# A two-layer decoder trunk on one Trainium2 core: the first two gate and up tile pairs by direct block products

## What is computed

```python
def rmsnorm(x, g):
    y = xf * lax.rsqrt(jnp.mean(xf * xf, axis=-1, keepdims=True) + EPS)
    return (y * g).astype(x.dtype)

def swiglu(x, wg, wu, wd):
    return (jax.nn.silu(x @ wg) * (x @ wu)) @ wd

h = h + 0.5 * swiglu(rmsnorm(h, norm_ffn1), ffn1_gate, ffn1_up, ffn1_down)   # 1024 -> 2816 -> 1024
```

## Time and profile before

| | |
|---|---|
| times of three runs | 2783.46, 2786.13, 2786.66 us |
| span of the profiled execution | 2784.5 us |
| TensorE busy | 2759.6 us, 99% of the span |
| VectorE busy | 1983.0 us, 71% |
| ScalarE busy | 1193.2 us, 43% |
| granted TensorE clock, mean | 0.999 |
| HBM read and written | 291.51 MB and 30.94 MB |

### The profile page before, as it was taken

One profiled execution on the slowest core, in us unless ns is written; L12 is line 12 of the kernel. 1 busy time (PEld: TensorE's weight loads), 2 busy tenths in 40 slices (PEclk: granted clock), 3 DMA queues, 4 the chain that ended last, 5 costly groups with the idle time before them and its releaser, 6 DMA issues.

```text
span 2784.5 us, 58089 instructions
## 1 busy us (share of the span) xinstructions
PE 2759.6 (99%) x22004; PEld 2677.3 (96%) x22004; DVE 1983.0 (71%) x3581; ACT 1193.2 (43%) x2139; POOL 128.3 (5%) x233
## 2 busy tenths in 40 slices
PE   8999999999999999999999999999999999999999
PEld 7999999998899999999999999999888999999999
DVE  8889534478767688887488895344787576899952
ACT  6445323435424254444254453234354333544521
POOL 0000001230000000000000000012300000000000
PEclk9999999999999999999999999999999999999999
DMA  4222325463335312223212222165723343122233
GB/s 140 92 96 96 108 75 198 158 203 127 108 109 191 122 61 91 90 91 121 84 69 90 90 105 100 68 206 159 226 107 119 106 179 130 62 96 100 99 106 104
DMA packets 104929, 326.02 MB, mean 117 GB/s; under 512 B 15055, under 2 KB 31967, under 8 KB 103216
## 3 DMA queue, kind: packets, MB, share of 16 engines
q1 hardware_dynamic: 91872, 280.75, 28.9%
q0 software_dynamic: 12880, 42.84, 4.7%
HBM read 291.51 MB, written 30.94 MB: 116 GB/s over the span
## 4 chain that ended last, share of the span: by engine, by line
PE 96%; DVE 2%; ACT 1%; issue 0%; DMA 0%; SPq 0%; DVEq 0%; ACTq 0%
PE ps L1442 51%; PE ps L1493 35%; PE ps L1679 3%; PE ps L1748 1%; PE ps L1961 1%; PE ps L1798 1%; PE ps L1779 1%; PE ps L1454 0%; PE ps L1826 0%; PE ps L1846 0%; PE ps L1730 0%; PE ps L1467 0%; DMA hT<-h_in 0%; PE ps L1788 0%; PE ps L1461 0%
## 5 line engine op out<-in xcount | busy, mean ns | idle before, releaser
L2121 DVE TENSOR_TENSOR w_lo<-w_raw,w_hi 128x1024 fp32r<-128x1024 f32 x240 | 292.7, 1223 | 345.2 <-ACT w_hi L829 341.6
L1493 PE MATMUL ps<-x_more,w_hi 128*128 128x296 f32 (+1 forms) x2112 | 456.8, 298 | 2.2 <-DVE x_more L2993 1.4
L1493 PE MATMUL ps<-x_hi,w_hi 128*128 128x296 f32 (+1 forms) x1408 | 420.5, 299 | 2.4 <-DVE w_lo L2159 2.4
L1493 PE MATMUL ps<-x_hi,w_lo 128*128 128x296 f32 (+1 forms) x1408 | 421.0, 299 | 0.0
L1493 PE MATMUL ps<-x_lo,w_hi 128*128 128x296 f32 (+1 forms) x1408 | 420.9, 299 | 0.0
L829 ACT ACTIVATE w_hi<-w_raw 128x1024 fp32r<-128x1024 f32 x224 | 235.0, 1053 | 407.2 <-PE ps L1442 240.1
L1442 PE MATMUL ps<-x_hi,w_hi 128*128 128x296 f32 (+1 forms) x1600 | 362.8, 308 | 3.8 <-ACT hT L1175 3.8
L2159 DVE TENSOR_TENSOR w_lo<-w_raw,w_hi 128x512 fp32r<-128x512 f32 x440 | 296.4, 689 | 88.9 <-ACT w_hi L877 86.5
L1493 PEld LDWEIGHTS ps<-x_more,w_hi 128*128 128x128 f32 x2112 | 350.7, 188 | 3.6 <-issue 2.1
L1442 PE MATMUL ps<-x_hi,w_lo 128*128 128x296 f32 (+1 forms) x1600 | 346.6, 298 | 0.0
L1442 PE MATMUL ps<-x_lo,w_hi 128*128 128x296 f32 (+1 forms) x1600 | 346.5, 298 | 0.0
(11 more groups left out here) (381 smaller groups left out, 4882.2 us busy)
## 6 DMA issues: line engine op xcount, KB each, us to landing
w_raw<-wstream SPq DMA_DIRECT2D x420, 512.0 KB, 3.8
kpage<-cache_k SPq DMA_DIRECT2D x128, 128.0 KB, 3.0
vpage<-cache_v POOLq DMA_DIRECT2D x128, 128.0 KB, 3.8
gate_rows<-hT SPq DMA_DIRECT2D x48, 296.0 KB, 3.0
d_sg<-gate_rows SPq DMA_DIRECT2D x16, 888.0 KB, 4.8
h_rows<-hT SPq DMA_DIRECT2D x2, 2368.0 KB, 9.6
hT<-h_rows SPq DMA_DIRECT2D x2, 2368.0 KB, 10.2
hT<-h_in SPq DMA_DIRECT2D x4, 592.0 KB, 8.4
```

Of the source, the lines that this page charges most:

```text
L1493: mm = pe.matmul(ps[:, bank, 0:span()], wp[:, k, :], xp, start=new and k == 0 and n == 0, stop=k == KH - 1 and n == 2, skip_group_check=True)
L2121: v.tensor_tensor(w_lo[:, slot, :, :], w_raw[:, slot, :, :], w_hi[:, slot, :, :].bitcast(F32), ALU.subtract).then_inc(weights_low, 1)
```

## The change

It touches layer 0's first SwiGLU alone.

- Pairs 0 and 1 are each made by direct block products: gate tile and up tile, 8 channel tiles, 3 passes, 2 token halves, 96 matmuls a pair in place of 84. For pair 0 this goes tile by tile (k = 0 to 7) as input tiles and weight pieces arrive. A new operand B12 is kept for it.
- The input is loaded tile by tile (8 loads in place of 4), and the first two weight units in four pieces that each hold two channel tiles of both (1024 contiguous bytes in place of 4096).
- The input array holds a second copy of h with tokens on partitions (five windows of 80 or 128 tokens by 1024). SP loads it behind the rest. ScalarE squares and sums its rows (an accumulator), takes Ln and Exp of the sums; VectorE multiplies an identity by them (diagonals), TensorE multiplies by ones to spread them over partitions, ScalarE copies the result out. The 14 matmuls on square_rooms and the 2 on ssum go.
- TensorE waits, ahead of pair 2's first product, for `pair_steps`, which VectorE's direct_rate(1) raises. Pair 2 then takes the seven-product scheme; pairs 2 and 3 stand written out, the loop starts at pair 4.
- POOL issues the constants after the input has arrived; the bias rows are made behind pair 2.

```diff
+DIRECT = 2
+            def load_chunk(c):
+                sp.dma_start(chunk(w_raw, c), wstream[0:2].rearrange("a p (k m) -> p a k m", k=8)[:, :, 2 * c:2 * c + 2, :]
+                             ).then_inc(chunk_load(c)[0], 16)
+            load_tile(0)
             sp.dma_start(prm[:, :], params[0][:, 0:NP_ - P]).then_inc(h_loaded[0], 16)
+            for c in range(4):
+                load_chunk(c)
+                load_tile(2 * c + 1)
+                if c < 3:
+                    load_tile(2 * c + 2)
+            load_first(2)
+            load_tokens(0)
+            load_first(3)
+            for w in range(1, WINDOWS):
+                load_tokens(w)
             sp.wait_ge(consts_loaded, 16 * CONSTS)
...
+            pl.wait_ge(h_loaded[3], TILE_COUNT[3])
+            pl.dma_start(ident[:, :], c_ident).then_inc(consts_loaded, 16)
...
+            def opening_inverse():
+                act.wait_ge(tokens_loaded, 16 * WINDOWS)
+                for w in range(WINDOWS):
+                    n = window(w)[1]
+                    act.activation(tokens[0:n, w, :], tokens[0:n, w, :], ACT.Square, accum_out=token_squares[0:n, w:w + 1]
+                                   ).then_inc(squared, 4 if w == WINDOWS - 1 else 1)
...
+            def opening_pairs():
+                for k in range(KD):
+                    for u in range(2):
+                        mm = direct_block(0, u, k)
+                        if k == KD - 1:
+                            mm.then_inc(products_done, 3 + u)
+                for p in range(1, DIRECT):
+                    for u in range(2):
+                        pe.wait_ge(weight_steps, W_STEPS * p + (W_STEPS if u else 5))
+                        if p == 1 and u:
+                            pe.wait_ge(norm_steps, 2)
+                        elif p > 1:
+                            pe.wait_ge(pair_steps, PAIR_STEPS * p + (6 if u else 4))
+                        for k in range(KD):
+                            if p == 1 and u == 0 and k == KD - 2:
+                                opening_inverse()
+                            mm = direct_block(p, u, k)
+                        mm.then_inc(products_done, 3 + u)
...
+                if opening:
+                    opening_pairs()
+                    pe.wait_ge(pair_steps, PAIR_STEPS * (DIRECT + 1) + 4)
+                    begin(DIRECT, DIRECT % 2)
+                    for n in range(DIRECT, 4):
+                        pair_(n, n % 2, "opening" if n == DIRECT else "steady")
+                        if n == DIRECT:
+                            bias_rows()
...
+            def opening_ffn():
...
+                diagonal_roots()
+                for k in range(KH):
+                    opening_low("T1", k, kept_rooms[:, k, 0, :], gain_of(P_GAIN, k))
+                v.wait_ge(norm_steps, 2)
+                direct_rate(0)
...
+                direct_gate(0)
+                direct_hidden(0)
...
+                for k in range(KH):
+                    opening_low("T2", k, difference_rooms(0, k)[0], None)
...
+                for k in range(KH):
+                    opening_low("T3", k, difference_rooms(0, k)[1], None)
...
+                sum_one(g, w_sum)
+                low(N, W_A11, g, w_sum)
...
+                sum_three(N, g)
+                low(N, W_S1, g, w_sum)
+                sum_two(N, g, w_sum)
+                sum_four(N, g, w_sum)
+                low(N, W_S2, g, w_sum)
+                for k in range(KH):
+                    fourth(0, k, P_GAIN, opened("T2", k))
+                low(N, W_S4, g, w_sum)
+                direct_rate(last)
+                for k in range(KH):
+                    opening_low("T4", k, difference_rooms(0, k)[0], None)
```

More of the change, by code:

```diff
@@ L993, in ffn @@
                 quad0 = l * QUADS + first // RING
-                pair_(N0, quad0, 0, "first", 0)
-                pair_(N0 + 1, quad0, 1, "steady", 1)
-                with act.Fori(1, KF // 2 - 1) as i:
+                opening = l == 0 and f == 0
+                if opening:
+                    opening_ffn()
+                    for n in range(DIRECT, 4):
+                        pair_(N0 + n, quad0 + n // 2, n % 2, "steady", n)
+                        if n == DIRECT:
+                            bias_rows()
+                else:
+                    pair_(N0, quad0, 0, "first", 0)
+                    pair_(N0 + 1, quad0, 1, "steady", 1)
+                with act.Fori(2 if opening else 1, KF // 2 - 1) as i:
                     for j in range(2):
@@ new lines, in opening_inverse @@
+            def opening_inverse():
+                pe.wait_ge(consts_loaded, 16 * CONSTS)
+                pe.wait_ge(squares_summed, 8)
+                for w in range(WINDOWS):
+                    c0, n = window(w)
+                    bank, c = (6, c0) if w < WINDOWS - 1 else (7, 0)
+                    mm = pe.matmul(ps[:, bank, c:c + n], ones[0:n, 0, :], diagonals[0:n, w, 0:n], start=True, stop=True)
+                mm.then_inc(square_total, 1)
+            def opening_pairs():
[11 more added lines that the diff above has]
+                            pe.wait_ge(pair_steps, PAIR_STEPS * p + (6 if u else 4))
+                        for k in range(KD):
+                            if p == 1 and u == 0 and k == KD - 2:
+                                opening_inverse()
+                            mm = direct_block(p, u, k)
+                        mm.then_inc(products_done, 3 + u)
@@ L1484, in ffn, with bias_rows @@
+            def bias_rows():
+                pe.wait_ge(bias_row_moved, 32)
+                for bank, c in ((2, 0), (3, 512), (6, 1024)):
+                    mm = pe.matmul(ps[0:16, bank, 0:min(512, RL - c)], rb[0:33, :], bucket[0:33, c:min(c + 512, RL)], start=True, stop=True)
+                mm.then_inc(bias_row_made, 1)
             def ffn(l, f, first):
@@ L1498, in operand @@
                     pe.wait_ge(weight_steps, W_STEPS * N + W_LOW[t])
+                opening = l == 0 and f == 0
                 def x_operand(t):
-                    pe.wait_ge(x_parts, parts(l, f, t, KH - 1))
+                    pe.wait_ge(x_parts, OPENING_PARTS.index((t, KH - 1)) + 1 if opening else parts(l, f, t, KH - 1))
                 def begin(N, j):
@@ L1509, in pair_ @@
                 def pair_(N, j, kind):
-                    first_ = kind == "first"
+                    first_ = kind in ("first", "opening")
                     operand(N, W_S1)
@@ L1545, in fifth @@
                         product(W_A12, BANK_B, True)
-                    if first_ and l == 0 and f == 0:
-                        opening_squares()
-                    if first_:
+                    if kind == "first":
                         fifth()
@@ L2092, in _ @@
             pe.sem_inc(units_multiplied, RING)
-            pe.wait_ge(bias_row_moved, 32)
-            for n, c in enumerate(range(0, RL, 512)):
-                mm = pe.matmul(ps[0:16, 5 + n, 0:min(512, RL - c)], rb[0:33, :], bucket[0:33, c:min(c + 512, RL)], start=True, stop=True)
-            mm.then_inc(bias_row_made, 1)
             for l in range(DEPTH):
@@ L3140, in layouts @@
     h = np.concatenate([a["x_sample"].reshape(TS, D), a["meta_tokens"], a["x_prompt"].reshape(SEQ, D)], axis=0)
-    out["h_in"] = h.T.reshape(KD, P, T).transpose(1, 0, 2)
+    rows = np.zeros((P, WINDOWS, D), f)
+    for w in range(WINDOWS):
+        c0, n = window(w)
+        rows[0:n, w] = h[c0:c0 + n]
+    out["h_in"] = np.concatenate([h.T.reshape(KD, P, T).transpose(1, 0, 2).reshape(P, KD * T), rows.reshape(P, WINDOWS * D)], axis=1)
     units = []
```

345 lines of the change are left out of this document (209 added, 136 removed).

## The result

| | before | changed |
|---|---|---|
| median of runs side by side | 2785.93 us (14 runs, 2782.93 to 2788.70) | 2792.45 us (14 runs, 2789.43 to 2794.73) |
| profiled execution: span | 2784.5 us | 2789.1 us |
| granted clock, mean of the span | 0.999 | 0.996 |

The ratio is 1.0026 with a 95% interval of 1.0019 to 1.0033: slower by 6.5 us in the median. That is more than the 5.6 us (0.2%) under which the prediction took a change for none, though the lower end of the interval, 0.19%, lies just under that mark. The prediction expected 2787.7 us, in a range of 2781.5 to 2792: 1.6 us slower than before. It was wrong: the median lies 0.45 us above its range, and the loss is four times the one that it forecast.

A forecast was written before the change was run, and what follows sets the result against it. TensorE, busy 99% of the span, was taken as the bound. Pair 2 beginning at 47.7 instead of 50.5 us (-2.8), bias rows +2.0 and lost clock +2.4 gave +1.6: 2787.7 us, range 2781.5 to 2792.

The forecast's parts named there:

- Landing: Arrival of the token windows that ScalarE's squares wait for: 7.5 MB by 21.7 us, plus 1.2, so 22.9 us.
- The other 5.2 at 408 GB/s: Opening loads: after 0.85 MB by 5 us and 1.46 more by 9, the remaining 5.2 MB arrive by 21.7 us.
- unknown of some 2 us in the landing: Allowance in the forecast's range for when the opening loads are seen to have arrived.
- it is covered: TensorE's wait for the diagonals may bring half speed, but pair 1 still ends before 47.7 us, so no cost.
- The first gap: TensorE's wait ahead of the spread, from 27.6 to 32.4 us, for the diagonals on VectorE: 4.8 us.
- VectorE's chain: VectorE's queued work from 34.4 us through the second rate: 13.3 us, releasing pair 2's first product at 47.7.
- rival 4: ScalarE's table switches each add a 1.28 us drain: chain 2.6 us longer, result +4.2, 2790.3 us; chance 0.03.
- The second gap: TensorE's wait ahead of pair 2's first product, 41.8 to 47.7 us: 5.9 us, plus 2.4 for lost clock.
- the first (clock kept): TensorE keeps full speed through the wait ahead of pair 2: -0.8 us, 2785.3 us; chance 0.28.
- Rival 2: The opening's waits don't bind and TensorE is the bound: pair 2 at 39.2 us, -11.3, 2774.8 us; chance 0.07.
- Rival 3: First weight units in 1024-byte runs load slowly, token windows land 5.5 us later: +7.1, 2793.2 us; chance 0.08.
- mixtures of small errors: Outcomes combining several small misses in the forecast's terms, anywhere in the opening; chance 0.07.

The follow-up runs named there:

- f12: The changed kernel with only 512 of 1024 columns of the second copy loaded and squared: 2786.17 us, ratio 1.0002 to the kernel before.
- e4: The changed kernel with both TensorE waits filled with matmuls whose result nobody reads (56 and 36): 2788.16 us, ratio 1.0009 to the kernel before.
- e1: The changed kernel with input tiles 1+2, 3+4 and 5+6+7 loaded by one DMA each: 2793.79 us, ratio 1.0026 to the kernel before.
- e2: The changed kernel with the first two weight units loaded whole, in 4096-byte runs: 2792.66 us, ratio 1.0023 to the kernel before.
- f9: The changed kernel with ScalarE and VectorE work reordered, four token windows squared while the fifth lands, spread behind 48 matmuls: 2787.22 us, ratio 1.0006.

## Why the prediction was wrong

The mechanism was right: TensorE waits twice, for the diagonals and for the second rate, and comes out of the second wait at half speed. Three terms failed.

- **Landing, mis-sized by 3.1 us.** "The other 5.2 at 408 GB/s": the rate of one window, 9 to 15 us, was carried over all that follows, where the changed kernel shows 296 to 393. 2.3 us are the rate and 0.7 the time from the last byte to the landing. f12 shows that bytes set the start. The 0.7 may lie with the next weights, which SP issues from 22.37 us on and which I had put at no cost; that is not shown. The "unknown of some 2 us in the landing" was too small a share of the range.
- **The spread, "it is covered".** The first gap was forecast at 4.8 us and was 8.1. I had written that it may bring half speed, but that TensorE would then still be in time. That looked at the matmuls behind the spread only. The spread itself stands between the diagonals and the first rate, ahead of VectorE's whole chain, and at half speed it takes 2.48 us for 1.2. So +1.3: 1.1 is the clock, as e4 shows (1.38 us at full speed, first rate 1.1 us sooner), and 0.2 that the spread takes 1.38 us for 1.2 even then.
- **VectorE's chain** from the first rate to the end of the second, 13.3, measured 13.8 (39.11 to 52.88): +0.5.

With +0.3 in small steps pair 2 begins at 52.93 in place of 47.7, 5.2 us late. Half speed behind it cost 17 matmul starts at 0.11 extra, 1.8 for the 2.4 charged: -0.6. The sum was +1.6; 1.6 + 5.2 - 0.6 = 6.2, and the milestone says 6.57; the last 0.4 us are not accounted for.

The other terms held: first matmul 6.15 (6.3), squares 25.96 to 31.27 or 5.3 (5.3), Ln and Exp 3.2 (3.1) with 1.30 from table load to Ln (31.28 to 32.58) and no drain, so rival 4 is false; diagonals 1.0 (1.1), bias rows 2.05 (2.0). The second gap, 5.6 (5.9) with its releaser as named, came out right because both of its ends, the end of pair 1 and the second rate, hang on the same late spread and were each more than 5 us late.

Of the rivals, the first (clock kept) is false: after 5.62 us of idleness matmuls start 0.25 us apart. The Trainium skill, page "TensorE: Matmul & The Clock Gate", section "What's actually happening", has idleness bring the half rate back, and the trace agrees at both gaps. Rival 2 (the waits don't bind) is false as well. Rival 3 named the right place, a late landing with the chain hanging on it, and a cause that the runs don't bear out: longer runs gained nothing in e1 and 0.8 us at most in e2. It had decided from 4 us of delay; 3.1 with the slow spread was enough. The combination of two moderate errors on one chain was left to 0.07 of "mixtures of small errors", although both raise the same chain.

What stays open: why the opening's loads run below the early rate. The dip to 296 GB/s at 14 to 17 us is not there when the constants come first (352), but then 17 to 22 us shows 287 for 386. Open too is what the next weights' loads cost the last token windows.

## What to carry to other kernels

When a reduction is moved from the engine that is the bound to a late load and a chain over three engines, the time is that of the last byte plus the chain, and the engine's saved work turns into waiting; price the load with the rate of the stretch in which it runs, over its whole length. A wait that gives TensorE half speed is charged twice: on the matmuls behind it, and on any short matmul group inside the chain that it waits for. Work that needs no late value belongs in front of the wait on each engine, but only if its own operands are there: a split that waited 3.4 us in front of the squares (f9) started them at 27.62 us, later than the 25.96 of the changed kernel.
